# A hybrid decoder step on one core: block ends without emptying GpSimd's transfers, one gate unit moved, two late waits and the norm sums reordered

## What is computed

```python
h = modulate(rmsnorm(x, norm1_g), shift1, scale1)
gq, gk, gv, gr, glr, aq, ak, av, ga, gb = split(h @ w_in)
y_a = (rmsnorm(gla(gq, gk, gv, glr, state)) * silu(gr)) @ w_branch_a      # branch A
y_b = dilated_attention_of_3_groups(aq, ak, av, caches) @ w_branch_b      # branch B
x = x + gate1 * ((sigmoid(ga) * y_a + sigmoid(gb) * y_b) @ w_out)
h2 = modulate(rmsnorm(x, norm2_g), shift2, scale2)
a, b = split(h2 @ w_up)
x = x + gate2 * ((silu(causal_conv3(a)) * b) @ w_down)
y = rmsnorm(x, normf_g)
```

## Time and profile before

| what | us |
|---|---|
| median of 3 runs (1249.87 to 1250.19) | 1250.01 |
| the profiled execution | 1249.03 |
| its span in the trace | 1247.3 |
| PE busy in the span | 1187.5 (95%) |
| DVE, ACT, POOL busy | 617.7, 447.0, 107.6 |
| stages, by the ends of the blocks: head and gla | 0 to 354.6 |
| att0; att1; att2 | to 499.2; to 601.8; to 704.8 |
| projections, w_out, second norm; FFN | to 842.3; to 1247.3 |

### The profile page before, as it was taken

The page is one execution under the profiler, slowest core; times in us unless marked ns, Lnnn a source line. Parts: engine busy times, 40 slices in busy tenths (PEclk is TensorE's granted clock), DMA queues, the critical chain, the costliest instruction groups (busy, mean ns, idle before and its releaser), DMA issues. The chain is left out here.

```text
span 1247.3 us, 23079 instructions
## 1 busy us (share of the span) xinstructions
PE 1187.5 (95%) x9681; PEld 1117.0 (90%) x9681; DVE 617.7 (50%) x999; ACT 447.0 (36%) x652; POOL 107.6 (9%) x189
## 2 busy tenths in 40 slices
PE   5899999999989999999997899999999999999997
PEld 3878998888889998989886799989999999999997
DVE  4432134645415544266586365548655655633333
ACT  3264333454434342343343353224333333222222
POOL 0000010111011001100310011000110110010000
PEclk9899999999989999999998999988999999999999
DMA  9664459773364224423437478613888887256661
GB/s 304 207 211 140 136 171 347 248 216 120 104 190 137 94 94 136 136 87 110 158 125 222 175 232 288 203 35 102 282 291 259 264 285 236 80 191 222 224 227 69
DMA packets 166016, 229.39 MB, mean 184 GB/s; under 512 B 7644, under 2 KB 148342, under 8 KB 164636
## 3 DMA queue, kind: packets, MB, share of 16 engines
q1 hardware_dynamic: 148720, 123.72, 32.5%
q10 hardware_dynamic: 1684, 54.56, 12.0%
q0 software_dynamic: 15536, 50.01, 11.8%
HBM read 204.58 MB, written 81.87 MB: 230 GB/s over the span
## 5 line engine op out<-in xcount | busy, mean ns | idle before, releaser
L378 PE MATMUL ps<-actH,whi 128*128 128x260 f32 x2064 | 433.9, 292 | 12.1 <-PEq L1245 4.8
L378 PE MATMUL ps<-actH,wlo 128*128 128x260 f32 x2064 | 418.2, 284 | 0.0
L378 PE MATMUL ps<-actL,whi 128*128 128x260 f32 x2064 | 417.6, 284 | 0.0
L378 PEld LDWEIGHTS ps<-actH,whi 128*128 128x128 f32 x2064 | 320.4, 191 | 32.4 <-issue 26.6
L378 PEld LDWEIGHTS ps<-actL,whi 128*128 128x128 f32 x2064 | 321.0, 190 | 0.0
L378 PEld LDWEIGHTS ps<-actH,wlo 128*128 128x128 f32 x2064 | 320.8, 190 | 0.0
L362 DVE TENSOR_TENSOR wlo<-wraw,whi 128x2048 fp32r<-128x2048 f32 (+2 forms) x95 | 141.3, 1499 | 157.1 <-ACT whi L349 156.8
L349 ACT ACTIVATE whi<-wraw 128x2048 fp32r<-128x2048 f32 (+2 forms) x95 | 119.3, 1275 | 133.0 <-PE ps L378 90.0
L433 ACT ACTIVATE arena<-ps 128x520 f32<-128x520 f32 x74 | 44.5, 601 | 208.1 <-PE ps L378 193.1
L378 PE MATMUL ps<-gH,whi 128*128 128x260 f32 x352 | 71.1, 283 | 0.0
L378 PE MATMUL ps<-gH,wlo 128*128 128x260 f32 x352 | 70.8, 282 | 0.0
(11 more groups left out here) (339 smaller groups left out, 1365.8 us busy)
## 6 DMA issues: line engine op xcount, KB each, us to landing
wraw<-in_w_in SPq DMA_DIRECT2D x38, 1024.0 KB, 5.4
out_win_s<-in_cache_win ACTq DMA_DIRECT2D x16, 2046.0 KB
wraw<-in_w_up SPq DMA_DIRECT2D x44, 512.0 KB, 5.8
out_win_s<-in_cache_win ACTq DMA_DIRECT2D x8, 2044.0 KB
wraw<-in_w_ada SPq DMA_DIRECT2D x14, 1024.0 KB, 6.2
arena<-in_w_ada SPq DMA_DIRECT2D x10, 1024.0 KB, 12.7
raw_gates<-arena SPq DMA_DIRECT2D x24, 260.0 KB, 6.9
arena<-raw_gates POOLq DMA_DIRECT2D x24, 260.0 KB, 4.2
```

Of the source, the lines that this page charges most:

```text
L378: last = pe.matmul(ps[:, 2 * (n % 2) + a, 0:HT], wt, X[:, k0 + j, a * HT:a * HT + HT], start=begin and j == 0 and wt is hi and X is H, sto ...
```

## The change

All six blocks get `no_gpsimd_drain=True`: POOL meets the others without waiting for its transfers to end. One unit of ga moves from `att0` (now 8 units, 32 places) to the middle of `att2` (now 5 units, 40 places). In the second norm, DVE adds the previous tile's square before it waits for the next tile. In the FFN, L2527 waits for one copy fewer, and the wait for all of `g_lo` moves into the first `down` tile, half by half. The last norm's sums go to PSUM bank 3 and become two rounds, with a wait for `ms_ready` put before the third turn; the store of y_sample moves from SP's queue to ACT's.

```diff
--- before.py
+++ after.py
@@ -102,9 +102,9 @@
         ada(N_HEAD + 1 + u)
 
     add("gr gr gr gr ga aq0 aq0 ak0 ak0 av0 av0", "gla")
-    add("aq1 aq1 ga ak1 ga ak1 av1 ga av1", "att0")
+    add("aq1 aq1 ga ak1 ga ak1 av1 av1", "att0")
     add("aq2 aq2 ak2 ak2 av2 av2", "att1")
-    add("gb gb gb gb", "att2")
+    add("gb gb ga gb gb", "att2")
     late = list(range(16, N_TAIL))
     for kind, src, n in (("bb", "w_branch_b", 2), ("ba", "w_branch_a", 4), ("wo", "w_out", 4)):
         for u in range(n):
@@ -555,11 +555,11 @@
                               ALU.add).then_inc(ada_read, 1)
 
 
-        def sums_pe(pe, bank, part, first):
+        def sums_pe(pe, bank, col, part, first):
 
             for n in range(5):
                 m = P if n < 4 else NS
-                last = pe.matmul(ps[0:m, bank, n:n + 1], part[:, P * n:P * n + m], ones[:, 0:1], start=first and n == 0,
+                last = pe.matmul(ps[0:m, bank, col + n:col + n + 1], part[:, P * n:P * n + m], ones[:, 0:1], start=first and n == 0,
                                  stop=not first and n == 4, skip_group_check=True)
             return last
 
@@ -1242,7 +1242,7 @@
             yield
             yield
 
-        with nc.Block() as block:
+        with nc.Block(no_gpsimd_drain=True) as block:
             @block.sync
             def _(sp):
                 head_sp(sp)
@@ -2241,9 +2241,9 @@
                     split_lo(dve, U[u]["i"] + 1)
                     for m in range(2):
                         n = U[u]["tile0"] + m
+                        square_dve(dve, 1, 2 * j + m - 1, n2)
                         dve.wait_ge(pass_done, passes[n])
                         residual_dve(dve, n, 2 * j + m, 2 * KD)
-                        square_dve(dve, 1, 2 * j + m - 1, n2)
                     late_ada_dve(dve, u)
                 ada_dve(dve, N_TAIL, ada4)
                 dch.link(dve, dve.memset(tok2["v"], 1.0))
@@ -2267,9 +2267,9 @@
                     late_ada_pe(pe, u)
                 ada_pe(pe, N_TAIL)
                 pe.wait_ge(s("sq_added"), KD - 2)
-                sums_pe(pe, 5, n2["t"], True)
+                sums_pe(pe, 5, 0, n2["t"], True)
                 pe.wait_ge(s("sq_ready"), KD)
-                sums_pe(pe, 5, n2["sq"][:, (KD - 1) % 2, :], False).then_inc(s("sq_summed"), 1)
+                sums_pe(pe, 5, 0, n2["sq"][:, (KD - 1) % 2, :], False).then_inc(s("sq_summed"), 1)
                 ada_pe(pe, N_TAIL + 1)
                 ada_turn_pe(pe, N_TAIL, ada4)
                 spread_root_pe(pe, 1, tok2)
@@ -2315,9 +2315,6 @@
                     if by_dve:
                         sp.wait_ge(s("y_tok_dve"), by_dve)
                     sp.dma_start(o["y_prompt"][P * n:P * n + P, :], yst[:, n, :]).then_inc(s("y_out"), 16)
-                sp.wait_ge(s("y_tok"), 5)
-                sp.wait_ge(s("y_tok_dve"), 5)
-                sp.dma_start(o["y_sample"], ysst).then_inc(s("y_out"), 16)
                 sp.wait_ge(s("y_out"), 80)
                 sp.wait_ge(outs, n_outs[0])
 
@@ -2385,6 +2382,9 @@
                     act.wait_ge(s("y_T"), turned)
                     act.activation(ytok(n, half), ps[rows, bank, :], ACT.Identity, scale=tok["r"][rows, n:n + 1])\
                        .then_inc(s("y_tok"), 1)
+                act.wait_ge(s("y_tok"), 5)
+                act.wait_ge(s("y_tok_dve"), 5)
+                act.dma_start(o["y_sample"], ysst).then_inc(s("y_out"), 16)
                 act.wait_ge(caches_moved, 16 * (len(moves) + 2 * NS))
                 assert n_moved[0] == len(moves)
 
@@ -2467,7 +2467,7 @@
                     residual_dve(dve, n, m, 5 * KD)
                 gain(KD - 1)
                 dve.wait_ge(s("sq_summed"), 2)
-                mean_dve(dve, ps[:, 1, YS:YS + 5], tok)
+                mean_dve(dve, ps[:, 3, YS:YS + 5], tok)
                 root_dve(dve, 2, tok)
                 dve.wait_ge(s("r_ready"), 3)
                 for n, bank, half, turned in YDVE:
@@ -2523,14 +2523,15 @@
                     unit(i, 1, False)
                     tail(i, 0, False)
                 pe.wait_ge(tile_read["act"], FA + KF - 1)
-                pe.wait_ge(s("tail_tok"), KF - 1)
+                pe.wait_ge(s("tail_tok"), KF - 2)
                 pe.transpose(ps[0:NS + 2, 7, 0:P], abuf[:, 1, TP:T + 2], ident).then_inc(s("tail_T"), 1)
-                pe.wait_ge(s("g_lo"), KF)
 
                 def down(m, i, first):
                     n = td0 + m
                     for half in range(2):
                         pe.wait_ge(lo_ready, vd0 + 2 * m + half + 1 + 4 * i)
+                        if m == 0 and first:
+                            pe.wait_ge(s("g_lo"), KF // 2 * (half + 1))
                         if half == 0 and first:
                             pe.wait_ge(tile_read[owner[n - 2]], freed[n - 2])
                         elif half == 0:
@@ -2554,22 +2555,16 @@
                 pe.wait_ge(s("gained"), KD - 1)
                 for n in range(3):
                     turn(n, range(KD - 1))
-                pe.wait_ge(s("x_new"), 2 * KD)
                 pe.wait_ge(s("sq_added"), 2 * (KD - 2))
+                sums_pe(pe, 3, YS, n3["t"], True)
                 pe.wait_ge(s("sq_ready"), 2 * KD)
-                last_sq = n3["sq"][:, (KD - 1) % 2, :]
-                for n in range(5):
-                    m = P if n < 4 else NS
-                    for x, part in enumerate((n3["t"], last_sq)):
-                        last = pe.matmul(ps[0:m, 1, YS + n:YS + n + 1], part[:, P * n:P * n + m], ones[:, 0:1],
-                                         start=x == 0, stop=x == 1)
-                last.then_inc(s("sq_summed"), 1)
+                sums_pe(pe, 3, YS, n3["sq"][:, (KD - 1) % 2, :], False).then_inc(s("sq_summed"), 1)
                 pe.wait_ge(s("gained"), KD)
                 for n in range(3):
+                    if n == 2:
+                        pe.wait_ge(s("ms_ready"), 3)
                     turn(n, [KD - 1]).then_inc(s("y_T"), 1)
-                turn(4, range(4))
-                pe.wait_ge(s("ms_ready"), 3)
-                turn(4, range(4, KD)).then_inc(s("y_T"), 1)
+                turn(4, range(KD)).then_inc(s("y_T"), 1)
                 for half in range(2):
                     pe.wait_ge(s("y_tok"), half + 1)
                     turn(3, range(4 * half, 4 * half + 4)).then_inc(s("y_T"), 1)
```

## The result

The changed kernel takes 1240.1 us (median of four runs, 1236.1 to 1241.2) where the kernel before took 1250.1 beside it: a ratio of 0.9909, 95% interval 0.9893 to 0.9926. (The quotient of the two medians is 0.9920, so steps of a tenth of a per cent between kernels are to be taken with care.) It is faster, but by 10.0 us where 19.5 were forecast, and 1240.1 lies above the range's upper end of 1237.0. The profiled execution took 1241.03 us, its span 1239.2.

The account below looks back on a forecast made before the run. PE bounds the kernel, through idle stretches and lower clock. Savings of 6.2 + 0.4 + 8.1 + 1.9 + 2.7 + 0.2 = 19.5 us take 1249.03 to 1229.5; with 1.0 for the median, 1230.5 us, range 1226.5 to 1237.0.

Parts of the forecast that it names:

- Blocks without the drain, 6.2: gla's end: 3.7 us less PE waiting without POOL's drain, plus 2.5 us of slow clock behind it; 6.2 us saved.
- att0, 0.4: att0 with 8 units: 1.1 us of L1613's wait saved, 0.7 lost to the last sample step; net 0.4 us saved.
- of the first kind: att0: even score steps at a unit's first and third place, where PE had no wait; 1.1 us saved.
- att2, 8.1: att2 with 5 units: L1900's 6.2 us, 1.5 of clock and 1.4 of other waits go, 1.0 comes; 8.1 us saved.
- The waits of L1613 for ACT stay: att2: PE's waits at L1613, some 0.5 us each, inside a pair of steps at neighbouring places, remain unchanged.
- the 3.9 us there stay: att2's end: set by SP after the last spilled tile lands, so the flag gives nothing and PE's 3.9 us remain.
- rival (a): att2: the spill's wait moves to the ga unit, costing 4.1 us plus 1.3 for the clock: 1235.9 us; chance 0.14.
- One sign by which I called the prediction wrong: att2: a raw_gates wait in the last three units would show the prediction wrong.
- Second norm, 1.9: Second norm: L562's 0.97 us wait for L611 goes and its 20 matmuls run faster; 1.9 us saved.
- FFN, 2.7: FFN: L2527 starts one transpose behind L2499 in place of 2.86 us; 2.7 us saved.
- Last norm and stores, 0.2: Kernel's end: the sums give 0, y_sample's store leaving SP gives 0.2 us.
- a long wait costs twice and a short one once: PE's waits: the clock falls behind long ones, about half rate, but stayed 1.00 after a wait of 2.6 us.

Follow-up runs that it names:

- e1: Kernel before with only the six block ends no longer waiting for GpSimd's transfers (no_gpsimd_drain=True); 1247.3 us, ratio 0.9966 to the kernel before.
- e4: Changed kernel with the ga unit back in att0, so every edit but the unit; 1242.9 us, ratio 0.9938 to the kernel before.
- f2: Changed kernel with att2's 39 steps one place later each (place 1 has none); 1234.7 us, ratio 0.9866 to the kernel before.
- h1: Changed kernel with only att2's steps from 23 on (the join and what follows) one place later; 1236.5 us, ratio 0.9882 to the kernel before.
- e3: Kernel before with only the edits of the second norm, the FFN and the last norm; 1245.8 us, ratio 0.9953 to the kernel before.
- g2: Changed kernel with y_sample's store back on SP's queue; 1240.3 us, ratio 0.9910 to the kernel before.
- g3: Changed kernel with the last norm's sums and turns as they were before; 1238.5 us, ratio 0.9900 to the kernel before.
- e2: Kernel before with only the ga unit moved from att0 to att2; 1248.2 us, ratio 0.9978 to the kernel before.
- f1: Changed kernel with att0's last eight steps (the sample keys) one place earlier; 1236.6 us, ratio 0.9884 to the kernel before.
- g1: f4 with the wait for att2's spilled tiles moved from SP at the block's end to ACT's first read; 1228.5 us, ratio 0.9812 to the kernel before.
- f3: Changed kernel with SP, in att2 alone, storing a unit's spilled tiles before issuing the next weights; 1238.4 us, ratio 0.9897 to the kernel before.
- f4: Changed kernel with the edits of f1, f2 and f3 together; 1231.1 us, ratio 0.9830 to the kernel before.

## Why the prediction was wrong

By its own steps:

- **Blocks without the drain, 6.2: right.** 3.6 in gla and, by e1 and e4, 2.4 in att0 by the clock.
- **att0, 0.4: half right.** The order "of the first kind" did free L1613, and the product and reduction behind the last matmul did hold up the end. They were put at 1.8 us and took 2.3. The step that failed is the clock: behind these 2.3 us it fell, and 1.5 us were lost in att1. I had taken the 2.6 us after which the earlier trace rows showed 1.00 as a bound below which a wait is free; one row could not bear that.
- **att2, 8.1: this term was mis-sized, and is half of the miss.** Its first reading, that the value loads hold up one spilled tile and that tile L1900, was right: 6.2 became 0.9 with 0.7 forecast. L1601's and L1894's 0.7 went too. What failed is "The waits of L1613 for ACT stay" and, for the end, "the 3.9 us there stay". I had read the new deal of steps against PE's order and SP's spills, and never against DVE's, where the pieces of `wlo` stand between the same places. Put against before: L1613 +1.3, `wlo` +1.3, the end +2.0, and the clock behind L1613's wait in place of that behind L1900's, so that most of the 1.5 counted for it did not come. In numbers: PE's idle time should have fallen by 6.6 us and fell by 2.3 (13.2 to 10.9), which is 4.3: the 1.3, 1.3 and 2.0, with 0.2 more at L1900, less the 0.3 counted for rival (a) and 0.2 at another wait that went. Its busy time should have grown by 10.0 (the unit's 11.5 less 1.5 for the clock) and grew by 11.2 (89.8 to 101.0), which is the other 1.2 of the 5.5. f2 and h1 took the causes apart, but for one: which of the two `wlo` pieces among the score steps makes L1613 wait was not tried.
- **Rival (a), the spill at the ga unit: not there.** The ga unit's first spill left at 655.7, and ACT took its buffer again at 666.7 without a wait. A wait like it came one unit later, on ACT and not on PE. In ACT's timeline of the changed kernel:

```profile
688.01 0.60 ACT L433 ACTIVATE arena<-ps 128x520 f32<-128x520 f32 x1 [13.37 <-DMA raw_gates<-arena]
```

The tile it waited for belongs to the fourth unit and was issued at 674.63, just behind a load of 1 MB (674.20) and one of 2 MB by POOL (673.87), and landed in 13.3 us, where the forecast had room for 9.7. The load by POOL (L2066, `gla_out`) is not in the prediction's count at all. PE waits for nothing between 674.23 and the block's end, so it cost nothing, against the 4.1 of the rival. One sign by which I called the prediction wrong is there, then, but is not what made it wrong. The Trainium skill's rule (DMA: Bandwidth & Descriptors, Queues, rings and completion order), that queues take turns packet by packet, would have given 7.5 us by my estimate; the landings here were 14.1 and 13.3, so an estimate by fair shares was too short both times.
- **Second norm, 1.9: right** (1.7 and 1.9 in after and e3), though its 20 matmuls took 2.3 us and not 2.0.
- **FFN, 2.7: right** for L2527 (2.86 to 0.11 behind L2499). The stage as a whole gained 2.1 in the changed kernel. 0.2 of the rest is the last part. Some 0.4 lies at the stage's start, where 17.7 us held 108 matmuls at a mean clock of 0.78 (836.6 to 854.3), and 110 at 0.82 before (842.3 to 860.0).
- **Last norm and stores, 0.2: nothing.** g2 and g3 put both edits at 0 within 0.2. The rule from the Trainium skill that only issuing time is saved (DMA: Bandwidth & Descriptors, Issuing engines are not separate DMA queues) agrees: even the 1.1 us of issue on SP were not saved, for they lie beside the prompt's stores.
- **The base.** The head took 219.1 us in the profiled execution of before and 219.9 to 223.4 in the thirteen others, e2 and e3 with the same code up to there among them. Its first loads landed later in after (the long run of products at L808 begins at 14.56 in place of 12.86), and the mean granted clock in the head was 0.96 in place of 0.97. The prediction has no term for the head, and so 2.8 us of the miss. A short execution to start from explains at least a part of them: I had measured it against the median of three runs, 1.0 above, and the larger groups, run later, put that median at 1251.3 to 1251.7, 2.3 to 2.7 above. The flag may have the rest. The three profiles without it have heads of 219.1, 219.9 and 221.6, the eleven with it 220.8 to 223.4. These ranges overlap, and which it is stays open.
- **Two readings and the range.** Step 16 is done after place 13 of the old deal and 16 of the new (`ceil(39 x 13/32)` and `ceil(39 x 16/40)` are both 16), not after 14 and 17. The spill at place 15 lies between them either way, so nothing hangs on it. The range's bad side was no sum of the bounds: added up like the good side (2.5 + 1.1 + 5.4 + 0.9 + 0.2 + 0.5, without the 3.3 for `wlo` in att0) they give 1241.1, and the measured 1240.1 would have lain inside.

In short: 5.5 for att2's order on DVE, 2.8 for the head (a short base, or in part the flag), 1.5 for the clock at att1, 1.6 for the rest, 11.4 of the span. The median missed by 9.6, since I had put it 1.0 above the profiled execution and it lay 0.9 below that of the changed kernel. f1 and f2 took 3 and 5 us back. The shown causes are those of att2 and att1; the head's is not.

## What to carry to other kernels

When steps are dealt anew over places, read the new deal against every engine's program, not only the one that is the bound: here a step moved by one place past a piece of weights on VectorE, and the cost came out two engines further, as a store that held up the end of the block. Set the base of a sum by several executions, and compare stage by stage. A wait for stores at a block's end belongs to the first reader of the data, if the bound engine does not need it (in g1 this took 1.5 us off PE's idle time).

## What the runs showed of the hardware that I had not expected

- **The clock after a wait of given length falls in some executions and not in others.** L2527's wait of 2.59 us was followed by 1.00 in the profile of before, and by a lower clock in e2 and in e1, here e1:

```profile
1104.67 0.27 PE L2527 MATMUL ps<-cst,arena 128*10 128x128 f32 x1 [2.59 <-DVE arena L2444]
...
1106.00:1108.00 2.00, 2.00 (x12) 2.00 (x11) 0.79 (x1) 0.00 (x0) 1.32 (x3) 0.50 1.29 491
```

The 2.2 or 2.3 us at att0's end were followed by a lower clock in after, f3, h1, g2 and g3, and not in e2 and f2. The wait of 1.7 or 1.8 at L1613 was followed by it in just those five, and not in e2 and f1, which has the same wait but a short one at att0's end. Right behind a wait of 1.2 us it never fell, in any of the fourteen profiles. Why the two places go together was not tried.
- **The clock also fell with no wait ahead of it.** The last unit of att2 in f2, where L1938 is L1935 of the changed kernel; the last wait of PE above 0.6 us was at 660.2:

```profile
685.58 1.95 PE L1938 MATMUL ps<-arena 128*128 128x4 f32 x16
...
684.00:687.60 3.60, 3.60 (x32) 3.44 (x31) 0.46 (x1) 0.03 (x1) 0.00 (x0) 1.00 0.48 147
688.00:690.00 2.00, 2.00 (x10) 1.78 (x9) 0.00 (x0) 0.00 (x0) 0.00 (x0) 0.50 0.82 317
```

PE counts as busy throughout. What it did before the fall were 24 small products of the samples, eight of 8x8 and sixteen of 128x4. In e1, e2, f1 and g3 the clock fell under the sixteen, in f2 and f4 within 1.1 us of their end, and in the other eight profiles it stayed at 1.00 until PE's last product of the stage. So the prediction's rule that a long wait costs twice and a short one once leaves out both this and the chance in it.
- **A store of 260 KB landed in 2.0, 2.5, 4.5 or 13.3 us**, by what had been issued ahead of it: a load of 1 MB some 5 us earlier (h1, before), the same 2.6 us earlier (after), or 3 MB within the last microsecond (after, at 674.6).
